# When VectorE splits its weight unit at the four meetings of half products

## The reference

```python
y = jnp.concatenate([y_a, y_b, y_c], axis=-1) @ w_out[l]
x = x + rmsnorm(y, g_post_mix[l])
h = rmsnorm(x, g_pre_ffn[l])
gate, up = jnp.split(h @ w_ffn_in[l], 2, axis=-1)
...
e = p[l] @ w_ple_up[l]
g = jax.nn.sigmoid(rmsnorm(x, g_ple_gate[l]) @ w_ple_gate[l])
x = x + rmsnorm(e * g, g_ple_post[l])
```

## Time and profile before

| | |
|---|---|
| median of 3 runs | 3285.89 us |
| profiled execution, its own time | 3286.9 us |
| its span | 3285.1 us |
| PE busy | 3234.1 us, 98% of the span |
| POOL busy | 1607.7 us, 49% |
| DVE busy | 1243.7 us, 38% |
| ACT busy | 1161.0 us, 35% |
| granted PE clock | 0.999 of full speed |
| chain that ended last | PE 92%, DVE 3%, POOL 2%, issue 2%, ACT 1% |

### The profile page before, as it was taken

How to read it: one execution, slowest core, us unless ns; L and a number is a source line. 1 busy time by engine, 2 the same in 40 slices (tenths; PEclk the granted TensorE clock), 3 DMA queues, 4 the chain that set the end, 5 groups by cost and what they waited for, 6 DMA issues and landing times.

```text
span 3285.1 us, 43101 instructions
## 1 busy us (share of the span) xinstructions
PE 3234.1 (98%) x15542; PEld 2634.7 (80%) x15542; DVE 1243.7 (38%) x2060; ACT 1161.0 (35%) x1838; POOL 1607.7 (49%) x841
## 2 busy tenths in 40 slices
PE   9999999999999999999999999999999999999998
PEld 7678888886788888888887778888888877688887
DVE  4753124567431245411445242124311443321134
ACT  4653222556532224422333432222322333332222
POOL 4546444765454447644465245444544453354444
PEclk9999999999999999999999999999999999999999
DMA  4112222221122222322222113222222221122221
GB/s 154 52 53 102 96 96 98 82 102 50 57 98 96 98 98 80 125 96 97 98 93 84 53 64 105 97 99 96 99 96 96 96 96 64 65 91 96 99 98 64
DMA packets 82397, 293.82 MB, mean 89 GB/s; under 512 B 9035, under 2 KB 11467, under 8 KB 82028
## 3 DMA queue, kind: packets, MB, share of 16 engines
q1 hardware_dynamic: 80944, 286.06, 25.6%
q10 hardware_dynamic: 1340, 6.23, 0.5%
HBM read 290.15 MB, written 2.10 MB: 89 GB/s over the span
## 4 chain that ended last, share of the span: by engine, by line
PE 92%; DVE 3%; POOL 2%; issue 2%; ACT 1%; DMA 0%; SPq 0%; DVEq 0%; POOLq 0%; ACTq 0%
PE bank L2108 28%; PE bank L2110 28%; PE bank L2109 28%; PE bank L2637 1%; PE bank L2617 1%; POOL w_lo L604 1%; POOL diag L739 1%; PE bank L2724 1%; PE bank L2479 0%; PE bank L2759 0%; PE bank L2439 0%; PE bank L2457 0%; PE bank L2121 0%; ACT y L1092 0%; PE bank L2909 0%
## 5 line engine op out<-in xcount | busy, mean ns | idle before, releaser
L604 POOL TENSOR_TENSOR w_lo<-w_raw,w_hi 128x1024 fp32r<-128x1024 f32 (+1 forms) x538 | 1300.4, 2421 | 1420.1 <-ACT w_hi L833 1376.0
L2108 PE MATMUL bank<-mvh,w_hi 128*128 128x512 f32 (+1 forms) x4454 | 1710.2, 384 | 11.3 <-DVE mvl L1439 2.9
L2110 PE MATMUL bank<-mvh,w_lo 128*128 128x512 f32 (+1 forms) x4454 | 1688.1, 379 | 0.0
L2109 PE MATMUL bank<-mvl,w_hi 128*128 128x512 f32 (+1 forms) x4454 | 1687.4, 379 | 0.0
L833 ACT ACTIVATE w_hi<-w_raw 128x1024 fp32r<-128x1024 f32 x537 | 568.1, 1059 | 1730.6 <-PE bank L2110 1715.9
L2108 PEld LDWEIGHTS bank<-mvh,w_hi 128*128 128x128 f32 x4454 | 837.8, 188 | 201.8 <-issue 35.2
L2110 PEld LDWEIGHTS bank<-mvh,w_lo 128*128 128x128 f32 x4454 | 837.6, 188 | 158.5
L2109 PEld LDWEIGHTS bank<-mvl,w_hi 128*128 128x128 f32 x4454 | 838.4, 188 | 150.9 <-issue 0.2
L1502 DVE TENSOR_TENSOR scr<-bank,rstd_b 128x512 f32<-128x512 f32 x264 | 181.4, 691 | 994.4 <-PE bank L2110 990.4
L1519 DVE TENSOR_TENSOR mvl<-big,mvh 128x512 fp32r<-128x512 f32 x132 | 270.1, 2056 | 346.6 <-ACT mvh L991 346.6
L739 POOL TENSOR_TENSOR diag<-diag,scr 128x256 f32<-128x256 f32 (+1 forms) x146 | 161.6, 1107 | 19.3 <-ACT scr L851 3.0
(11 more groups left out here) (221 smaller groups left out, 1665.7 us busy)
## 6 DMA issues: line engine op xcount, KB each, us to landing
w_raw<-in_weights SPq DMA_DIRECT2D x537, 512.0 KB, 3.2
x<-in_x SPq DMA_DIRECT2D x8, 256.0 KB, 8.7
out_y<-y SPq DMA_DIRECT2D x8, 256.0 KB, 2.2
tab<-in_dist ACTq DMA_DIRECT2D x2, 640.0 KB
tab<-in_gmlp ACTq DMA_DIRECT2D x2, 640.0 KB
tab<-in_ret_dil ACTq DMA_DIRECT2D x1, 1280.0 KB
y<-in_p ACTq DMA_DIRECT2D x2, 512.0 KB, 3.5
y<-in_rotary ACTq DMA_DIRECT2D x1, 1024.0 KB
```

Source lines behind the costliest of these rows:

```text
L604: last = nc.gpsimd.tensor_tensor(w_lo[:, slot, at], w_raw[:, slot, at], w_hi[:, slot, at].bitcast(F32), ALU.subtract)
L2108: nc.tensor.matmul(bank[:, at], hi, mvh[:, k, at], start=first, stop=False, skip_group_check=again)
L2109: nc.tensor.matmul(bank[:, at], hi, mvl[:, k, at], start=False, stop=False, skip_group_check=again)
L2110: return nc.tensor.matmul(bank[:, at], lo, mvh[:, k, at], start=False, stop=last, skip_group_check=again)
```

## The change

`low_weights` moves from ahead of the first half's tiles to behind the update (and `beside`) of its fourth tile, k = 3, ahead of `low` of tile 2. POOL's wait for it with its memset moves behind one more `add_squares`.

```diff
@@ second_half, POOL
                 splits(u0 + 1)
+                add_squares(name, post + 3, post + 4)
                 split_by_dve(RING + SPLIT_POST.index(name))
-                add_squares(name, post + 3, post + 4)
                 split_in_pieces()
@@ enter_halves, DVE
                 L = lin[name]
-                low_weights(L.u0 + 1)
-
                 def low(k, half):
...
                             update(k, half)
                             if half == 0:
                                 beside(k)
+                        if half == 0 and k == 3:
+                            low_weights(L.u0 + 1)
                         if k:
                             low(k - 1, half)
```

## The result

The changed kernel takes 3290.38 us (median of 20 runs, 3288.98 to 3291.75), the one before in the same runs 3286.08 us. The ratio of the two is 1.0013, with a 95% interval of 1.0007 to 1.0019: 4.3 us longer, clear of the measurement, and under the 0.2% that I had called no difference. Forecast were 3290.6 us, 4.7 us longer.

A forecast was written before the change was run, and what follows sets the result against it. PE was taken as the bound, busy 3234.1 of 3285.1 us, so only its waits count. 2 x 0.24 (output) + 2 x 2.12 (gate) = 4.7 us on the median of 3285.89 gave 3290.6 us, range 3287.2 to 3292.6.

The forecast's parts named there:

- part 1: Output meeting, ahead of the updates: POOL's root takes 0.71 instead of 1.62 us, and PE's 0.90 us wait goes.
- first rival: Output meetings: root stays at 1.62 us for its own reason, +1.14 us each, 3292.4 us in all; chance 0.09.
- part 2: Output meeting, DVE: L1418 ends at 238.37, `low` follows at once, PE gets tile 2 1.3 us earlier, its 0.66 us gone.
- part 3: Output meeting, POOL: memset waits for L1418, first piece at 238.50, chain 6.59 us; +0.24 us per meeting.
- part 4: Gate meeting, DVE: updates some 0.2 us earlier, PE's tile 1 wait about 0.6 us shorter, tile 2 0.6 us later.
- part 5: Gate meeting, POOL: first piece follows L1418 at 667.20 instead of 665.08, chain 6.59 us; +2.12 us per meeting.
- The three steps of PE's waits: Gate meeting: PE feels POOL's later first piece three times, at the low parts of units 1, 2 and 3.
- part 6: All four meetings: the moved square costs nothing, running in POOL's idle time; weight loads up to 4 us later, harmless.
- part 7: Behind the meetings: all is relative to PE; 0 us given back, at most 0.5 per meeting.
- the second: Rival for the four meetings: POOL's pieces do not decide, -2.3 us in all, 3283.6 us; chance 0.07.
- The third: Rival: gate meetings' 2.12 us partly given back, -1.0 to -3.0 us on the sum, say 3288 us; chance 0.10.
- the sum of 4.7: Whole kernel: 2 x 0.24 us at output meetings plus 2 x 2.12 us at gate meetings, 4.7 us longer.

The follow-up runs named there:

- y2: Kernel before, but VectorE's subtraction left out at the four meetings and GpSimd splitting unit 1 itself in one instruction; 3287.75 us, ratio 1.0005.
- x1: Changed kernel with VectorE's move alone, GpSimd's square staying behind the memset; 3293.73 us, ratio 1.0023 to the kernel before.
- x4: Changed kernel with GpSimd's wait and memset between the two pieces of unit 2 instead of ahead of both; 3287.96 us, 1.0005 to the kernel before.
- y3: Changed kernel with the subtraction done twice, the second waiting for the first; 3296.58 us, ratio 1.0032 to the kernel before.
- y4: Changed kernel with the subtraction behind the third tile's update (k = 2) instead of the fourth; 3286.34 us, ratio 1.0000 to the kernel before.

## Why the prediction was right, and where it was off

1. **The root, part 1.** Predicted 0.71 instead of 1.62 us and PE's 0.90 us gone; measured 0.71 us, and the spread starts 2.16 us behind the transpose instead of 3.07. The rule of the Trainium skill that the prediction drew on (SBUF — State Buffer, section Who interferes with whom) agrees with it, and again with y2's first `low` of 1.97 us. The first rival is out.

2. **VectorE at the output meeting, part 2.** L1418 was to start 6.56 us behind the transpose (237.15 - 230.59); it started at 6.61. Tile 2's `mvl` followed at once, and no wait of PE for it is left (0.66 us before).

3. **POOL at the output meeting, part 3.** First piece predicted at 7.91 us (238.50 - 230.59), measured 7.93. The chain behind it was predicted at 6.59 us and took 6.47: the first pair took 2.87 us, not 2.98, and the square between 0.73, not 0.92, while the second pair took 2.90 and not 2.72. The `low` cut in at other places than I had laid them. Hence +0.14 and not +0.24 us.

4. **VectorE at the gate meeting, part 4.** Updates predicted 2.62 us behind the transpose, measured 2.63; first `low` 0.47 us, as predicted. L1418, though, started at 8.36 and not 8.03 (665.85 in the old time): the updates had become early enough to run into another wait, the 0.24 us of L2013 at 663.51 for PE's L2110, since `beside` at tile 2 needs the last product of the gate. I had read this instruction as one without a wait, which it was before. It starts 0.65 us behind the update ahead of it, where it was 0.33, and that is the whole difference. For the same reason PE's wait for tile 1 shrank by 0.23 us, to 0.56, and not by 0.6, and tile 2's `low` ended 0.9 us later than before, not 0.6.

5. **POOL at the gate meeting, part 5.** First piece predicted at 9.38 us, measured 9.69, for the reason just given; the chain 6.59 against 6.46. Together +2.30 instead of +2.12 us. The three steps of PE's waits are there, 1.25, 0.88 and 0.47 us. The output meetings have three as well (0.29, 0.72 and 0.48), where I had written of one, 0.6 us at unit 3. In all four meetings they add up to 8.2 us, where I had written some 10.

6. **The square, part 6,** costs nothing where it is now, but it was not idle in the change: x1 shows that without it the change would have cost 0.7 us more per meeting. My sentence was right of the kernel predicted, and said less than there was. The weight load behind unit 1's slot was issued 4.9 us later at the output meeting (8.14 us behind the transpose instead of 3.24), not 4; between 225 and 1345 us ACT waits for no load in either kernel, so this cost nothing, as I had said.

7. **Behind the meetings, part 7.** I counted nothing given back. The meetings' sum is 4.86 us, yet from the first meeting's transpose (0.96 us earlier in this profile, before anything that was changed) to the end the kernel is 4.5 us longer (3.5 + 0.96). Between the meetings some 0.1 us each is won; from which wait I have not traced.

Of the rivals, the second (3283.6, the pieces do not decide) fails by x4 and y3. The third was right in kind, some 0.4 us being given back, and wrong in size. The mechanism came out as predicted. That the sum of 4.7 came within 0.4 us of the measured 4.3 is in part luck: it was 0.2 too much at the output meetings and 0.35 too little at the gate meetings, and it left out the 0.4 given back. Each of these is small beside the 2.3 us of a gate meeting, whose chain was right.

## What to carry to other kernels

Before work is moved behind a busy engine's list, look who waits for it in order: here a semaphore that counts units in order, and a wait at the head of POOL's list, put two later units behind one that nobody needed early. Read for each place the latest of all that release the chain, not the wait that the move removes: the same move gained 0.9 us of root time and lost it again, and one or two places earlier it would have kept it. Places that look alike need their own answer; of the places tried, the output meetings want the subtraction behind tile 1 or 2, the gate meetings want it where it was.

## What the runs showed of the hardware

- GpSimd and VectorE, both reading two inputs in SBUF, held each other up until the running instruction had ended. A power of 128x2 took 1.62 us beside VectorE's 128x1024 subtraction and ended 0.57 us behind it; alone it took 0.71. A `low` of 0.47 us took 1.97 us beside GpSimd's 128x1024 subtraction and ended 0.28 us behind it.
- PE's granted clock fell from 1.00 to 0.50 for some 3 us after it had waited 0.63 and 1.48 us with 0.6 us of work between the two (y2), in both gate meetings, and after 2.51 us in y3, in both. It did not fall behind 1.25 and 0.88 us (changed), behind 1.56 and 0.88 (y3, output meetings) or behind 1.69 (y4, gate meetings). In x1 it fell in one gate meeting and not in the other, though PE had waited the same 0.55 and 1.25 us ahead of it in both, and in the changed kernel, where it did not fall. It cost nothing there, since PE had to wait for `w_lo` anyway. So the waits alone do not decide, and another execution of one of these kernels may differ from its profile in this. Stretches of x1 over the two meetings, granted clock 0.83 and 1.00:

```profile
664.00:674.00 10.00, 7.79 (x50) 6.99 (x48) 9.76 (x18) 5.44 (x12) 6.72 (x7) 0.83 0.40 139
1324.00:1336.00 12.00, 8.17 (x62) 7.36 (x62) 11.54 (x22) 6.11 (x13) 8.46 (x9) 1.00 0.35 124
```

What tells these cases apart is left open.
